# Queries, keys and gates of the second network: hi and lo halves of the normed input streamed in one 512-column matmul

## What is computed

```python
oa = moba_attention(rope_partial(heads(qa), pos), rope_partial(heads(ka), pos), heads(va)) * jax.nn.silu(ga)
ob = dsa_attention(rope_partial(heads(qb), pos), rope_partial(heads(kb_), pos), heads(vb_), qi, ki, wi) * jax.nn.silu(gb)
oc = forgetting_attention(heads(qc), heads(kc), heads(vc), log_f) * jax.nn.silu(gc)
```

## Time and profile before

| what | value |
|---|---|
| median of 3 runs | 1073.27 us (1071.59 to 1073.71) |
| profiled execution | 1073.57 us, span 1071.6 us |
| PE busy | 1050.7 us, 98% |
| DVE busy | 733.7 us, 68% |
| ACT busy | 591.6 us, 55% |
| granted TensorE clock, mean | 0.995 |

### The profile page before, as it was taken

The page is one execution under the profiler, slowest core; times in us unless marked ns, Lnnn a source line. Parts: engine busy times, 40 slices in busy tenths (PEclk is TensorE's granted clock), DMA queues, the critical chain, the costliest instruction groups (busy, mean ns, idle before and its releaser), DMA issues.

```text
span 1071.6 us, 18030 instructions
## 1 busy us (share of the span) xinstructions
PE 1050.7 (98%) x6797; PEld 885.6 (83%) x6797; DVE 733.7 (68%) x1577; ACT 591.6 (55%) x1209; POOL 2.6 (0%) x10
## 2 busy tenths in 40 slices
PE   5999999999999999999999999999999999999997
PEld 3677776788997779989898988889988898888886
DVE  4635567666597756787778766658788778765665
ACT  4534245543265446567766764445567677665444
POOL 0000000000000000000000000000000000000000
PEclk9999999999999999999999999999999999999999
DMA  9997651222342324565555466666464545555662
GB/s 326 337 319 235 182 182 40 60 60 62 97 122 66 80 69 125 147 171 143 137 142 153 144 168 184 191 193 177 131 175 138 139 138 158 156 161 176 195 211 84
DMA packets 203550, 165.41 MB, mean 154 GB/s; under 512 B 7100, under 2 KB 172712, under 8 KB 203464
## 3 DMA queue, kind: packets, MB, share of 16 engines
q1 hardware_dynamic: 202944, 163.28, 52.0%
q0 software_dynamic: 192, 0.66, 0.2%
q10 hardware_dynamic: 328, 0.32, 0.1%
HBM read 163.18 MB, written 1.05 MB: 153 GB/s over the span
## 4 chain that ended last, share of the span: by engine, by line
PE 92%; DVE 4%; ACT 1%; issue 1%; DMA 0%; ACTq 0%; DVEq 0%
PE pj L2072 24%; PE pj L2074 23%; PE pj L2073 23%; PE pj L2166 1%; PE tr L2623 1%; DVE w_lo L1338 1%; PE ac L2427 1%; PE ac L2562 1%; PE sc L2271 1%; PE tr L2278 1%; PE sc L2413 1%; PE ac L2292 1%; PE sc L2544 1%; PE sc L2542 1%; ACT w_hi L835 1%
## 5 line engine op out<-in xcount | busy, mean ns | idle before, releaser
L1338 DVE TENSOR_TENSOR w_lo<-raw,w_hi 128x1024 fp32r<-128x1024 f32 (+2 forms) x258 | 309.4, 1202 | 143.0 <-ACT w_hi L835 141.9
L835 ACT ACTIVATE w_hi<-raw 128x1024 fp32r<-128x1024 f32 (+2 forms) x258 | 268.0, 1040 | 91.0 <-PE pj L2074 87.4
L2072 PE MATMUL pj<-h_hi,w_hi 128*128 128x256 f32 (+1 forms) x960 | 299.6, 312 | 0.2
L2074 PE MATMUL pj<-h_hi,w_lo 128*128 128x256 f32 (+1 forms) x960 | 291.8, 304 | 0.0
L2073 PE MATMUL pj<-h_lo,w_hi 128*128 128x256 f32 (+1 forms) x960 | 291.6, 304 | 0.0
L2072 PEld LDWEIGHTS pj<-h_hi,w_hi 128*128 128x128 f32 x960 | 184.1, 192 | 19.2 <-issue 10.4
L2074 PEld LDWEIGHTS pj<-h_hi,w_lo 128*128 128x128 f32 x960 | 184.2, 192 | 7.5
L2073 PEld LDWEIGHTS pj<-h_lo,w_hi 128*128 128x128 f32 x960 | 184.4, 192 | 6.3
L2072 PE MATMUL pj<-w_hi,h_hi 128*128 128x512 f32 x344 | 137.4, 399 | 2.8 <-DVE w_lo L1338 1.6
L2074 PE MATMUL pj<-w_hi,h_lo 128*128 128x512 f32 x344 | 134.2, 390 | 0.0
L2073 PE MATMUL pj<-w_lo,h_hi 128*128 128x512 f32 x344 | 134.2, 390 | 0.0
(11 more groups left out here) (358 smaller groups left out, 1472.7 us busy)
## 6 DMA issues: line engine op xcount, KB each, us to landing
raw<-in_w_in_dram SPq DMA_DIRECT2D x152, 512.0 KB, 3.8
ada_raw<-in_ada_w_dram SPq DMA_DIRECT2D x48, 512.0 KB, 7.6
raw<-in_even_w_in_dram SPq DMA_DIRECT2D x28, 512.0 KB, 5.2
raw<-in_w_branch_dram SPq DMA_DIRECT2D x24, 512.0 KB, 3.7
raw<-in_w_out_dram SPq DMA_DIRECT2D x16, 512.0 KB, 3.8
raw<-in_odd_w_in_dram SPq DMA_DIRECT2D x11, 512.0 KB, 4.0
raw<-in_even_w_out_dram SPq DMA_DIRECT2D x8, 512.0 KB, 3.7
raw<-in_odd_w_out_dram SPq DMA_DIRECT2D x8, 512.0 KB, 3.8
```

The costliest lines, as they stand in the source:

```text
L835: last = nc.scalar.activation(hi, src, ACT.Copy)
L1338: last = nc.vector.tensor_tensor(lo, src, hi.bitcast(F32), ALU.subtract)
L2072: nc.tensor.matmul(dst, lh, rh, start=first, stop=False)
L2074: return nc.tensor.matmul(dst, ll, rh, start=False, stop=final)
```

## The change

`is_folded` names the q, k and g chunks of the second network. For them h_hi and h_lo become two halves of one tile h_both, and a term of the product is one matmul of 512 columns, w_hi times [h_hi, h_lo], and one of 256, w_lo times h_hi, added to the first half of the bank. The bank's two halves are then added on the way out. For q and k ACT copies the first half as before (signal part_set) and DVE adds the second to the copy, ahead of the rotation; DVE gives back the bank. For a gate ACT copies the first half to ntmp (`gate_copy`, signal gate_part), DVE adds the second (`gate_sum`), and tanh is taken of the sum in ntmp. In a slot that drains a gate, ACT does gate_copy, the split, then tanh; DVE does gate_sum, the split, then the two gate products, and in a pair slot gate_sum stands between the head scores and the split, the products after the reciprocals.

```diff
--- before.py
+++ after.py
@@ -132,6 +132,12 @@
     return out + [("out", m) for m in range(KT)]
 
 
+def is_folded(name, i):
+
+
+    return name in ("q", "k", "g")
+
+
 def chunk_groups(name, i):
 
     if name in VALUE_NAMES:
@@ -139,6 +145,8 @@
     last = {"au": "act", "bq": "act", "bk": "act", "az": "dve", "bz": "dve", "eout": "dve",
             "ckv": "act", "kr": "act", "cq": "act", "cz": "dve", "oout": "dve",
             "qi": "act", "q": "act", "k": "act", "g": "dve", "out": "dve"}
+    if is_folded(name, i):
+        return [(name, i, "dve")]
     if name == "wkv":
         keys = [("kn", 4 * i + j, "dve" if 4 * i + j in DVE_KEYS else "act") for j in range(4)]
         return keys + [("vm", (i, t), "dve") for t in range(4)]
@@ -212,6 +220,7 @@
 LAST_GROUP = [LAST_OF_CHUNK1.get(c, -1) for c in range(CB)]
 VALUE_CHUNKS = [c for c, x in enumerate(L0_CHUNKS) if x[0] in VALUE_NAMES]
 LAST_GROUP += [GB + lay * NG2 + LAST_OF_CHUNK2.get(c, -1) for lay in range(LAYERS_2) for c in range(C2)]
+FOLDED_QK = [c for c, x in enumerate(B2_CHUNKS) if is_folded(*x) and x[0] != "g"]
 PARTIALS = [c for c, x in enumerate(B2_CHUNKS) if is_partial(*x)]
 assert C2 % NRAW == 0 and C2 % NSPLIT == 0 and NG2 % NBANK == 0
 
@@ -427,7 +436,8 @@
         m_hi, m_lo = sb("m_hi", [P, KT * TOK], F32R), sb("m_lo", [P, KT * TOK], F32R)
         cond32 = sb("cond32", [P, KT, 32])
         x_t = sb("x_t", [P, KT, TOK])
-        h_hi, h_lo = sb("h_hi", [P, KT, TOK], F32R), sb("h_lo", [P, KT, TOK], F32R)
+        h_both = sb("h_both", [P, 2, KT, TOK], F32R)
+        h_hi, h_lo = h_both[:, 0], h_both[:, 1]
         raw = sb("raw", [P, NRAW, WEL])
         w_hi, w_lo = sb("w_hi", [P, NSPLIT, WEL], F32R), sb("w_lo", [P, NSPLIT, WEL], F32R)
         work = sb("work", [P, 12288])
@@ -577,6 +587,7 @@
         sc2_done, neg_set, exp2_set, prob2_set, pv2_done, o2_set = (
             sem("sc2_done"), sem("neg_set"), sem("exp2_set"), sem("prob2_set"), sem("pv2_done"), sem("o2_set"))
         recip_set = sem("recip_set")
+        part_set, gate_part = sem("part_set"), sem("gate_part")
         og_set, g_hi_set, g_lo_set = sem("og_set"), sem("g_hi_set"), sem("g_lo_set")
         mg_set, mg_lo = sem("mg_set"), sem("mg_lo")
         x_turned, x_copied, gain_in, out_used = sem("x_turned"), sem("x_copied"), sem("gain_in"), sem("out_used")
@@ -1166,16 +1177,20 @@
                         src = bank(g)[:, 0:SEQ]
                         if kind in ("y", "out"):
                             continue
-                        proj_ready(act, g, lay)
+                        if kind == "g":
+                            act.wait_ge(*freed_at(g, lay))
+                        else:
+                            proj_ready(act, g, lay)
+                        signal = part_set if is_folded(kind, i) else freed["act"]
                         if kind == "qi":
                             nc.scalar.activation(qi_h[:, i, :], src, ACT.Copy).then_inc(freed["act"], 1)
                         elif kind in ("q", "k"):
                             scale = QK_SCALE if kind == "q" else 1.0
                             if BRANCH_ORDER[i // 4] == FORGET:
                                 dst = q_h if kind == "q" else k_h
-                                nc.scalar.activation(dst[:, i % NQK, :], src, ACT.Copy, scale=scale).then_inc(freed["act"], 1)
+                                nc.scalar.activation(dst[:, i % NQK, :], src, ACT.Copy, scale=scale).then_inc(signal, 1)
                             else:
-                                h_rope_input(rope_free(i), kind == "k", scale, src)
+                                h_rope_input(rope_free(i), kind == "k", scale, src, signal)
                         elif kind == "v":
                             b, n = i
                             if b:
@@ -1183,10 +1198,11 @@
                             nc.scalar.activation(v_h[:, n, :], bank(g), ACT.Copy).then_inc(freed["act"], 1)
                         elif kind == "g":
                             if i >= 2:
-                                act.wait_ge(*freed_at(G2_OF[("g", i - 2)], lay))
+                                act.wait_ge(og_set, lay * NTRIP + i - 1)
                             if i < 2:
                                 act.wait_ge(is_acc, lay * 16 + (12 if i == 0 else 16))
-                            nc.scalar.activation(tanh[:, i % 2, 0:SEQ], src, ACT.Tanh, scale=0.5).then_inc(tanh_set, 1)
+                            nc.scalar.activation(tanh[:, i % 2, 0:SEQ], ntmp[:, 2 * (i % 2), :], ACT.Tanh, scale=0.5)\
+                                .then_inc(tanh_set, 1)
                         elif kind == "merge":
                             b, half, n = i
                             q = 3 * half + b
@@ -1195,10 +1211,17 @@
                             nc.scalar.activation(gate_h[:, gate_slot(b, half, n), :], bank(g), ACT.Tanh, scale=0.5)\
                                 .then_inc(freed["act"], 1)
 
-                def h_rope_input(n, place, scale, src):
+                def gate_copy(c):
+                    i = B2_CHUNKS[c][1]
+                    proj_ready(act, G2_OF[("g", i)], lay)
+                    if i >= 2:
+                        act.wait_ge(og_set, lay * NTRIP + i - 1)
+                    nc.scalar.activation(ntmp[:, 2 * (i % 2), :], bank(G2_OF[("g", i)])[:, 0:SEQ], ACT.Copy).then_inc(gate_part, 1)
+
+                def h_rope_input(n, place, scale, src, signal):
 
                     act.wait_ge(rope_out, ROPES1 + lay * ROPES2 + n)
-                    nc.scalar.activation(rope[:, int(place), :], src, ACT.Copy, scale=scale).then_inc(freed["act"], 1)
+                    nc.scalar.activation(rope[:, int(place), :], src, ACT.Copy, scale=scale).then_inc(signal, 1)
 
                 def h_turned(use):
                     kind, i = TR2[use]
@@ -1243,12 +1266,17 @@
                         i = B2_CHUNKS[s - 2][1]
                         act.wait_ge(og_set, lay * NTRIP + i + 1)
                         nc.scalar.activation(g_hi[:, i, :], ntmp[:, 2 * (i % 2) + 1, :], ACT.Copy).then_inc(g_hi_set, 1)
-                    if 1 <= s <= B2_IN:
+                    gate = 1 <= s <= B2_IN and B2_CHUNKS[s - 1][0] == "g"
+                    if gate:
+                        gate_copy(s - 1)
+                    elif 1 <= s <= B2_IN:
                         h_evacuate(s - 1)
                     if s == MISC_SLOT and lay + 1 < LAYERS_2:
                         misc_split_hi(lay + 1)
                     if 1 <= s <= B2_IN:
                         split_hi(pos(s, lay) + AHEAD)
+                    if gate:
+                        h_evacuate(s - 1)
                     if s == LOG_SLOT:
                         act.wait_ge(fx_set, lay + 1)
                         after(nc.scalar.activation(lfa, lf, ACT.Abs))
@@ -1827,16 +1855,21 @@
                 def h_evacuate(c):
                     for kind, i, _ in chunk_groups(*B2_CHUNKS[c]):
                         g = G2_OF[(kind, i)]
+                        if kind in ("q", "k") and is_folded(kind, i):
+                            dve.wait_ge(part_set, lay * len(FOLDED_QK) + FOLDED_QK.index(c) + 1)
+                            if BRANCH_ORDER[i // 4] == FORGET:
+                                dst = (q_h if kind == "q" else k_h)[:, i % NQK, :]
+                            else:
+                                dst = rope[:, int(kind == "k"), :]
+                            nc.vector.scalar_tensor_tensor(dst, bank(g)[:, SEQ:TOK], QK_SCALE if kind == "q" else 1.0, dst,
+                                                           ALU.mult, ALU.add).then_inc(freed["dve"], 1)
                         if kind == "k" and BRANCH_ORDER[i // 4] != FORGET:
                             dve.wait_ge(*freed_at(g, lay))
                             rotate_two(rope[:, :, :], qk_h[:, i % NQK, :, :], pr_cos, pr_sin, PR_SHUFFLE)
                         elif kind == "g":
-                            proj_ready(dve, g, lay)
+                            a, b = ntmp[:, 2 * (i % 2), :], ntmp[:, 2 * (i % 2) + 1, :]
                             dve.wait_ge(tanh_set, 16 + lay * NTRIP + i + 1)
-                            a, b = ntmp[:, 2 * (i % 2), :], ntmp[:, 2 * (i % 2) + 1, :]
-                            nc.vector.scalar_tensor_tensor(a, tanh[:, i % 2, 0:SEQ], 1.0, bank(g)[:, 0:SEQ], ALU.add,
-                                                           ALU.mult).then_inc(freed["dve"], 1)
-                            dve.wait_ge(*freed_at(g, lay))
+                            after(nc.vector.scalar_tensor_tensor(a, tanh[:, i % 2, 0:SEQ], 1.0, a, ALU.add, ALU.mult))
                             dve.wait_ge(o2_set, lay * NTRIP + i + 1)
                             nc.vector.scalar_tensor_tensor(b, a, 0.5, o_h[:, i, :], ALU.mult, ALU.mult).then_inc(og_set, 1)
                         elif kind == "y":
@@ -1861,6 +1894,14 @@
                             proj_ready(dve, g, lay)
```

(30 more changed lines are left out.)

## The result

The changed kernel takes 1086.88 us (median of 4 runs, 1086.53 to 1087.37) against 1072.43: ratio 1.0134, 95% interval 1.012 to 1.0147. Its profiled execution took 1087.37 us, with a span of 1085.4, 13.8 us more than before. First the page, against the earlier trace rows: the busy time of each engine, then the engines' shares of the chain that ended last.

A forecast was written before the change was run, and what follows sets the result against it. The prediction took TensorE (PE, busy 98% of the span) as the bound. Stalls less saving gave 1073.57 + 5.9 + 6.9 = 1086.4, less 0.3 for the median: 1086 us; likeliest case 1082 to 1090, full range 1068 to 1092.

The forecast's parts named there:

- the gates' detour: Pair slots 21, 29, 37, 45: exps queue behind tanh, which waits for DVE's sum; exps +1.46 us, probabilities some 1.2 later.
- PE's saving: Folded q, k, g chunks on PE: 0.013 us saved per term, 0.104 per chunk, 7.5 us in all.
- The borders: Where 256- and 512-column matmuls meet: start to start 0.12 us for 256 then 512, 0.22 for 512 then 256.
- DVE's and ACT's added work: Per layer 24 q/k and 12 gate sums, about 13 us of DVE; 12 gate copies, 3.4 us of ACT.
- Chunk 8: Two sums ahead of w_lo of chunk 8 on DVE put +0.8 us straight onto the path.
- DVE's lateness: Second layer: DVE's scores late by 1.8 us at slot 17, growing to 8.5 at slot 49.
- The stalls: PE stalls at chunks 8 and 36 and slots 22, 30, 34, 38, 46, 50; 9.2 us in the second layer.
- PE's saving set against the stalls: Second layer: 32 chunks x 0.104 = 3.3 us against stalls of 9.2, net +5.9.
- the wide matmul does not save: Rival: a term stays at 0.360 us, so only stalls remain; 1088 to 1091; chance 0.12, including sums dearer than 0.40.
- the cover holds: Rival: DVE and ACT absorb the sums in their waits; 3 to 5 us gained, 1068 to 1070; chance 0.18.

The follow-up runs named there:

- wide_only: Kernel before, with q, k and g on one 512- and one 256-column matmul a term, drains unchanged, right bank halves never added; 1066.83 us, ratio 0.9946.
- no_q0k1: Changed kernel with its first four projections q0, k0, q1, k1 left unfolded; 1084.54 us, ratio 1.0113.
- tanh_late: Changed kernel with ACT's tanh moved behind the four exps in the four pair slots that drain a gate; 1079.70 us, ratio 1.0066.
- gates_tanh_late: Changed kernel with only the gates folded and, in the four pair slots, tanh behind the exps; 1072.08 us, ratio 0.9996.
- sums_only: Changed kernel's drains with the 256-column matmuls of the kernel before, sums adding the left half again; 1087.72 us, ratio 1.0131.
- selective2: Changed kernel folding all but q0, k0, k1, k3, k6, k9 and gates 0, 2 to 6, 10, 11; 1069.04 us, ratio 0.9971.

## Why the prediction was right, point by point

The number was right (1086 forecast, 1086.88 measured), and so was the mechanism: late drains and the gates' detour make PE stall by more than it saves. That the number came out within 1 us is partly luck. In the second layer the forecast was 9.2 of stalls less 3.3 saved, the ledger has 7.8 less 1.8: each term was off by some 1.4 us, and the errors cancelled to 5.9 against 5.97. In the first layer they did not (6.9 against 7.65).

- *PE's saving* was too large. Over 70 folded chunks, first start to last start plus 0.227, the mean is 2.835 us against 2.911 before (the last matmul counted with 0.120): 0.076 a chunk, not 0.104, 5.5 us in all, not 7.5. The borders were single transitions. In a running stream 512 to 256 takes 0.23 to 0.24 and 256 to 512 takes 0.11 to 0.12, as the rows from 778.47 on show. The best chunks take the 2.78 forecast, 0.10 less than their 2.88 before; others save only 0.04 to 0.07. From start to start even less arrives: 4.55 us in wide_only, after 0.33 lost at chunk 8. The Trainium skill's rule ("TensorE: Matmul & The Clock Gate", "Wait — 56ns, not 53.3ns?") would save 1.4 us; the measured value, 4.4 at equal clock in wide_only, does not agree with it.
- *DVE's and ACT's added work* was right: 25.9 us against some 25, and the sums take 0.417 us each (L1864 and L1903 both).
- *Chunk 8*: 0.8 forecast, 0.97 and 0.94 measured; no_q0k1 confirms its cause.
- *The detour*: exps +1.46 forecast, +1.50 at slot 37. tanh_late and gates_tanh_late show it at work.
- *DVE's lateness*, second layer, forecast and measured: slot 17 1.8 and 1.87, 21 2.2 and 2.20, 29 2.3 and 1.80, 33 4.5 and 3.31, 37 4.7 and 4.26, 41 5.9 and 5.45, 45 7.0 and 6.46, 49 8.5 and 7.67.
- *The stalls*: those of slots 22, 30, 34 and 46 were set too high, in sum by some 1.7 us in the second layer (4.4 against 2.65). Missed were chunks 12 and 19 (0.57 together): I had not made the index scores wait for the rotation of their queries, which stands behind q and k sums on DVE (chunk 12's stall is gone in no_q0k1, chunk 19's is not). Missed as well was the ACT copy that ends the wait in slot 22. The first layer's 43, 61 and 62 (0.8) were missed too.
- *PE's saving set against the stalls* was 3.3 us a layer; the stalls of the second layer sum to 7.8 and the net is 5.97, so 1.8 shows between the stalls. But sums_only, without any saving on PE, loses 6.23 there: the faster PE makes the stalls themselves larger, and 0.3 is all that the saving is worth. For the same reason the rival *the wide matmul does not save* was priced too high: the kernel that it describes is sums_only, priced by that rival at 1088 to 1091 and measured at 1087.72, less than 1 us from the changed kernel. The time of the changed kernel alone could not have told that rival from the forecast; wide_only and the 2.78 us chunks do.
- *Rivals*: the cover holds for q and k away from chunks 8, 12, 19 and slot 38, but not with the gates' detour, which is where that rival said it would be decided: at slot 21 the scores were 2.20 us late, not under 1.

Left open: why some folded chunks take 2.78 us and others up to 2.92. The same chunks vary before the change too, from 2.86 to 2.98, so the spread does not come from folding alone. Open too is why the first layer stalls before chunk 61 and the second does not.

## What to carry to other kernels

An engine with a quarter of its time free can still be the bound when its order is written out: count how late its deliveries come against each margin, not how busy it is. When a drain goes from one engine to two, look for what stands behind the new wait in program order; putting that one wait behind work others need was worth 6.5 us here, with no instruction saved. Look as well for waits that close into a ring between two engines. A saving that needs extra work elsewhere should be taken chunk by chunk, where the margins hold it.

## What was not expected of the hardware

The spans of some profiled executions differ by 1.5 us ahead of any folded chunk, where slot 0 ends. The stretch 440 to 442 us, columns as in the earlier trace rows with the granted clock as the first figure behind POOL, in the kernel before and in wide_only:

```profile
440.00:442.00 2.00, 2.00 (x12) 2.00 (x11) 1.66 (x11) 0.00 (x0) 0.00 (x0) 0.50 0.00 0
```
```profile
440.00:442.00 2.00, 2.00 (x18) 1.84 (x17) 1.73 (x10) 0.02 (x1) 0.00 (x0) 1.00 0.00 0
```

In the first PE had the lower of its two levels, 1.2 GHz, for this stretch and issued 12 matmuls where the other issued 18. Ahead of it stand 8 matmuls of one column (from 438.39, 1.03 us in all), but the same 8 stand in wide_only (from 437.71, 1.03 us as well), and there the clock stayed at 1.00; so they do not settle it, and the cause is open. The fall came in nine of the twelve profiled executions, the changed kernel's among them. In wide_only, gates_tanh_late and selective2 it did not, so 1.5 us of their profiled spans is not the edit's. The table's sums begin at chunk 4, behind it.

The timed executions fall into two groups as well, by the mean granted clock of the whole execution; whether this fall is what parts them no trace shows. Beside wide_only, the kernel before takes 1073.4 us (median of 12) at 0.995 or 0.996 and 1071.0 (median of 5) at 0.998 or 0.999. A median depends on how many executions of each group it has. Compared within a group, each with the executions of before beside it, wide_only is 4.4 us faster than before, selective2 2.4 (2.8 for its one execution at the lower value), gates_tanh_late 0.6 to 0.7 slower, and the changed kernel, all of whose executions had the lower value, 13.5 slower than the 1073.4. The ledger's -4.55, -2.87, +0.42 and +13.62 agree with these better than the ratios of all executions do.
